# The first two tiles of the feed-forward block's closing projection: one after the other, or side by side

## The chip, the cores and the metric

The kernel runs on one NeuronCore of a Trainium2 chip. The metric is the device time of one execution in microseconds (us), lower is better. TensorE multiplies matrices, VectorE and ScalarE work elementwise, GpSimd here only subtracts, SyncE issues the weight loads.

## What is computed

Two layers of a streaming encoder over 640 tokens (512 of a prompt and 8 streams of 16), width 1024. Each layer holds two half-step feed-forward blocks (FFN) around a mixer:

```
def half_swiglu(x, g, w_up, w_down):
    h = rms_norm(x, g)
    a, b = jnp.split(h @ w_up, 2, axis=-1)
    return x + 0.5 * ((jax.nn.silu(a) * b) @ w_down)

def layer(x, ...):
    x = half_swiglu(x, ffn1_norm, ffn1_up, ffn1_down)
    ...   # sparse attention and a gated convolution, gated, projected, added to x
    x = half_swiglu(x, ffn2_norm, ffn2_up, ffn2_down)
```

`w_down` is 2816 x 1024. The change concerns the last part of `(silu(a) * b) @ w_down`, which is run four times: twice in each layer.

## The kernel before

All values are kept feature-major: 128 features on the partitions, the 640 tokens along the free axis, as two halves of 320. Matrix products are computed in float32 precision from two fp32r parts of each operand: `passes` issues, for one block of 128 x 128 weights, three products (hi x hi, hi x lo, lo x hi) over both halves, so six matmuls. The hidden width of 2816 is 22 blocks. The first 18 are handled by jobs with a seven-product scheme (`jobs`, `product`, names M1 to M7), which TensorE, ScalarE and VectorE work off in an order written out by hand. The last four blocks of the hidden width (`LAST` = 4, `LAST_AT` = 18) are added by plain tiles: this is the closing projection, called "closing" below. It has eight tiles (`KB` = 8), one for each 128 output features, and each tile sums four blocks: 4 x 6 = 24 matmuls into the PSUM buffer `lin[0]` (even tiles) or `lin[1]` (odd tiles).

Around the closing each engine follows its own written order, and semaphores join them:

- **TensorE** (`ffn`, lines 995 to 1005) runs a loop of four rounds with two tiles each. Before a tile it waits until the tile two back has left PSUM (`evacuated`) and until the tile's weights are there in both parts (`lo_ready`). In even tiles it also waits, before the third and the fourth block, for the hidden block itself (`g_ready`). The fourth hidden block is the last thing that the jobs make: VectorE's `lo_g` (line 2045) writes its low part `g_lo`.
- **ScalarE** (`closing`, line 1272) does for each tile j: `split` (line 1252) the weights of tile j + 2 into `w_hi`, then wait for `x` of tile j, then write the high part of the next norm's input `h_hi` (line 1257) and the square `sq` (line 1266). The weights have two buffers, so tile k + 2 overwrites the buffer of tile k:

```
            def split(L, k, i=0, step=2, cols=KB * P):
                s = k % 2
                act.wait_ge(tile_done.sem, L * TILES + (k - 1) + (step * i))
                ...
                nc.scalar.activation(w_hi[:, s, 0:cols], w_raw[:, s, 0:cols], ACT.Copy).then_inc(hi_ready.sem, 1)
```

- **GpSimd** (`low`, line 588) then subtracts, `w_lo = w_raw - w_hi`, and signals `lo_ready`.
- **SyncE** (`load`, line 528) loads `w_raw` of tile k once `w_lo` of tile k - 2 is made.
- **VectorE** (`closing`, line 1856) does for each tile: add it to `x` out of PSUM (line 1868), make `h_lo` (line 1821), and add `sq` into `acc` (line 1832). In the last closing of all, `h_hi` and `h_lo` fall away. In the second closing (layer 0, second FFN) VectorE and ScalarE also prepare the first job of the next layer in between: after tile 3 VectorE adds two weight strips (`add_strips` S1, S2, line 1907), after tile 4 two more (S3 and `first_fourth`), and ScalarE writes their high parts (line 1308).

After tile 7 comes the next stage's first tile, whose weights (1024 columns) go through the same `split` and `low`.

Of the kernel before, what the change touches and what calls it, by code (L numbers as in the profile page):

```python
# [37 lines left out]
KB = D_MODEL // P  # L38
TT = T // P
FB = D_FF // P  # L40
# [15 lines left out]
LAST = GROUPS[SPLIT_GROUPS]  # L56
LAST_AT = FB - LAST
# [119 lines left out]
def build(nc, wts, x_in, gains_in, cos_in, sin_in, ident_in, bmask_in, convw_in, state_in,  # L177
          kcache_in, vcache_in, kidx_in, y_out, k_out, v_out, ki_out, conv_out):
    ctx = ExitStack()
    with ctx:  # L180
# [109 lines left out]
        last_hi = [g_hi[:, i, :] for i in range(LAST)]  # L290
        last_lo = [g_lo[:, i, :] for i in range(LAST)]
# [46 lines left out]
        def res(slot):  # L338
            return lin[slot][:, :, 0:HALF]
# [16 lines left out]
        lo_ready = Signal("lo_ready", TILES)  # L356
        tile_done = Signal("tile_done", TILES)
        evacuated = Signal("evacuated", RESULTS, 2)
# [37 lines left out]
        g_ready = Signal("g_ready", 2 * FB)  # L396
# [319 lines left out]
        def _(pe):  # L716
            def passes(out, s, c, rhs_hi, rhs_lo, first, last):

                whi, wlo = w_hi[:, s, c * P:(c + 1) * P], w_lo[:, s, c * P:(c + 1) * P]
                for n, (w, a) in enumerate(((whi, rhs_hi), (whi, rhs_lo), (wlo, rhs_hi))):  # L720
                    for half in range(2):
                        ins = nc.tensor.matmul(out[:, half, :], w, a[:, half * HALF:(half + 1) * HALF],  # L722
                                               start=first and n == 0, stop=last and n == 2)
                return ins

            def linear(L, n, m, s, hi, lo, blocks=KB, before_last=None, out=None, after_block=None, frees_rows=False):

                out = res(s) if out is None else out

                pe.wait_ge(evacuated.sem, evacuated.count(L, m - 1))  # L730
                pe.wait_ge(lo_ready.sem, lo_ready.count(L, n + 1))
                for c in range(blocks):
                    if before_last and c == blocks - 1:
                        before_last()
                    ins = passes(out, s, c, hi[:, c, :], lo[:, c, :], c == 0, c == blocks - 1)
                    if after_block:
                        after_block()
                    if frees_rows and c == 3:
                        ins.then_inc(first_rows_free.sem, 1)
                ins.then_inc(tile_done.sem, 1)  # L740

            def first_linear(L, n, m, p):


                s = n % 2
                pe.wait_ge(evacuated.sem, evacuated.count(L, m - 1))
                pe.wait_ge(lo_ready.sem, lo_ready.count(L, n + 1))
                for c in range(KB):
                    if c == SUM_BEFORE:
                        sum_squares(L, p)  # L750
                    pe.wait_ge(h_ready.sem, h_ready.count(L, (p - 1) * KB + c + 1))
                    ins = passes(res(m % 2), s, c, h_hi[:, c, :], h_lo[:, c, :], c == 0, c == KB - 1)
                ins.then_inc(tile_done.sem, 1)
# [94 lines left out]
            def second_linear(L, n, m, p):  # L848

                blocks = iter(range(KB))  # L850

                def after_block():
                    if next(blocks) == SPREAD_AFTER:
                        spread_r(L, p)
                linear(L, n, m, n % 2, h_hi, h_lo, out=res(m % 2), after_block=after_block)
# [113 lines left out]
            def jobs(L, f, q, m):  # L969

                first_job(L, f, q, m)
                for k in range(2, NJ):
                    m1(L, q + k)
                    m4(L, q + k - 1)
                    m6(L, q + k)
                    m3(L, q + k - 1)
                    m2(L, q + k)
                    m7(L, q + k)
                    m5(L, q + k)
                m4(L, q + NJ - 1)  # L980
                pe.wait_ge(g_made.sem, g_made.count(L, ups(f, NJ - 2)))
                m3(L, q + NJ - 1)

            def ffn(L, f, n0, m0):
                q = f * NJ
                if L == f == 0:
                    opening_pair()
                else:
                    first_linear(L, n0, m0, (0, 2)[f])
                    second_linear(L, n0 + 1, m0 + 1, (0, 2)[f])  # L990
                for k in range(2, 2 * PLAIN):
                    linear(L, n0 + k, m0 + k, k % 2, h_hi, h_lo, frees_rows=k == 2 * PLAIN - 1)
                n0, m0 = n0 + 2 * PLAIN, m0 + 2 * PLAIN
                jobs(L, f, q, m0)
                with pe.Fori(0, KB // 2) as i:

                    pe.wait_ge(g_ready.sem, g_ready.count(L, f * FB + FB - 2))
                    for s in range(2):
                        pe.wait_ge(evacuated.sem, evacuated.count(L, m0 + s - 1 + 2 * i))
                        pe.wait_ge(lo_ready.sem, lo_ready.count(L, n0 + s + 1 + 2 * i))  # L1000
                        for c in range(LAST):
                            if s == 0 and c >= LAST - 2:
                                pe.wait_ge(g_ready.sem, g_ready.count(L, f * FB + LAST_AT + c + 1))
                            ins = passes(res(s), s, c, last_hi[c], last_lo[c], c == 0, c == LAST - 1)
                        ins.then_inc(tile_done.sem, 1)

# [104 lines left out]
            for _ in range(WARM_UP):  # L1111
                nc.tensor.matmul(bank[:, 3, :], ones[:, 0:1].to_broadcast([P, P]), ones[:, 0:1].to_broadcast([P, 512]),
                                 start=True, stop=True)
            for L in range(DEPTH):
                ffn(L, 0, FFN1_AT, 0)

                first_linear(L, MIX_AT, MIX_RES, 1)
# [112 lines left out]
                with pe.Fori(0, KB // 2) as i:  # L1230
# [5 lines left out]
                    for s in range(2):  # L1236
                        linear(L, OUT_AT + s + 2 * i, OUT_RES + s + 2 * i, s, m_hi, m_lo,
                               before_last=last_sum if s == 0 else None)
                ffn(L, 1, FFN2_AT, FFN2_RES)

            sum_last_squares()
# [1516 lines left out]
```

## Time and profile before

| | |
|---|---|
| device time, median of 3 runs | 2693.67 us (2692.46 to 2694.69) |
| the profiled execution: its own time | 2693.38 us |
| its span, first to last instruction | 2691.6 us |
| mean granted TensorE clock | 0.998 |
| TensorE busy | 2649.7 us (98%) |
| VectorE, ScalarE, GpSimd busy | 2050.8, 1347.4, 1014.6 us |

The profiled execution's own time is 1.8 us more than its span, for what lies before the first and after the last instruction. The trace names instructions by engine, line and tile. Matmuls overlap: one takes 0.31 us from start to end, but they start 0.147 us apart, so a duration is read from starts. A line "x2" of the timeline merges two matmuls. The closings begin at 409.55, 1315.50, 1741.08 and 2647.03 us of the span.

### The profile page before, as it was taken

To read this page: it belongs to the slowest core of one execution; us is meant where nothing else is said; L and a number is where in the kernel's file an instruction comes from. 1 tells how busy PE (TensorE), PEld (TensorE's weight loads), DVE (VectorE), ACT (ScalarE), POOL (GpSimd) and SP (SyncE) were. 2 spreads that over 40 slices of the span, in tenths; PEclk is the share of its full clock that TensorE was granted. 3 is DMA by queue.
4 is the path that set the end of the run, shared out by engine and by line. 5 is a ranking of instruction groups with operands and counts; after the bars stand their busy time and mean duration, and the time that the engine had idled before them with its cause. 6 is when DMAs were issued, how large, how long until landed. Compare 5 with 4: busy or idle time off the path is not lost. (4 is left out here: it accounts for less than half of the span.)

```text
span 2691.6 us, 48351 instructions
## 1 busy us (share of the span) xinstructions
PE 2649.7 (98%) x18372; PEld 2584.3 (96%) x18372; DVE 2050.8 (76%) x3441; ACT 1347.4 (50%) x2498; POOL 1014.6 (38%) x690
## 2 busy tenths in 40 slices
PE   9999999999999999999999999999999999999997
PEld 8999999998999999999999999998989999999997
DVE  8998976886433699989689889668773347989985
ACT  5555555636322355555545555464463224555553
POOL 2343333345433333343333433333544333343432
PEclk9999999999999999999999999999999999999999
DMA  3222223233222222232212222222332221222222
GB/s 120 79 95 92 74 79 98 88 126 126 64 70 94 70 68 98 69 104 80 79 65 93 77 98 79 76 92 89 133 111 71 70 94 63 77 97 79 91 83 71
DMA packets 89783, 234.27 MB, mean 87 GB/s; under 512 B 8816, under 2 KB 42352, under 8 KB 89072
## 3 DMA queue, kind: packets, MB, share of 16 engines
q1 hardware_dynamic: 74784, 204.11, 23.0%
q10 hardware_dynamic: 14800, 27.51, 3.0%
q8 instruction: 125, 2.05, 0.3%
q14 instruction: 74, 0.61, 0.1%
HBM read 223.32 MB, written 8.27 MB: 86 GB/s over the span
## 5 line engine op out<-in xcount | busy, mean ns | idle before, releaser
L588 POOL TENSOR_TENSOR w_lo<-w_raw,w_hi 128x1024 fp32r<-128x1024 f32 (+1 forms) x190 | 403.3, 2123 | 679.4 <-ACT w_hi L1252 663.5
L642 POOL TENSOR_TENSOR lo_A<-raw_odd,hi_A 128x512 fp32r<-128x512 f32 (+1 forms) x180 | 277.5, 1541 | 476.9 <-ACT hi_A L1308 476.6
L1252 ACT ACTIVATE w_hi<-w_raw 128x1024 fp32r<-128x1024 f32 (+1 forms) x174 | 168.7, 970 | 470.7 <-PE lin L722 341.5
L642 POOL TENSOR_TENSOR lo_A<-raw_even,hi_A 128x512 fp32r<-128x512 f32 (+1 forms) x180 | 247.4, 1375 | 399.9 <-ACT hi_A L1308 398.8
L722 PE MATMUL lin<-h_hi,w_hi 128*128 128x320 f32 x1600 | 374.6, 315 | 5.0 <-DVE tmp L1808 2.7
L722 PE MATMUL lin<-h_hi,w_lo 128*128 128x320 f32 x1600 | 365.2, 309 | 0.0
L722 PE MATMUL lin<-h_lo,w_hi 128*128 128x320 f32 x1600 | 364.8, 309 | 0.0
L722 PEld LDWEIGHTS lin<-h_hi,w_hi 128*128 128x128 f32 x1600 | 265.6, 189 | 18.6 <-issue 14.0
L722 PEld LDWEIGHTS lin<-h_lo,w_hi 128*128 128x128 f32 x1600 | 267.9, 188 | 0.0
L722 PEld LDWEIGHTS lin<-h_hi,w_lo 128*128 128x128 f32 x1600 | 267.8, 188 | 0.0
L887 PE MATMUL bank<-h_hi,hi_A 128*128 128x320 f32 x704 | 217.8, 309 | 1.1 <-DVE h_lo L2058 0.7
L887 PE MATMUL bank<-h_hi,lo_A 128*128 128x320 f32 x704 | 217.5, 309 | 0.0
L887 PE MATMUL bank<-h_lo,hi_A 128*128 128x320 f32 x704 | 217.5, 309 | 0.0
L1308 ACT ACTIVATE hi_S<-lin 128x512 fp32r<-128x512 f32 (+1 forms) x240 | 130.3, 553 | 127.9 <-DVE lin L1907 65.8
L1917 DVE TENSOR_TENSOR lo_S<-lin,hi_S 128x512 fp32r<-128x512 f32 (+1 forms) x240 | 150.6, 629 | 13.0 <-ACT hi_S L1308 11.2
L887 PE MATMUL bank<-T_hi,hi_S 128*128 128x320 f32 x480 | 148.4, 309 | 1.0 <-DVE lo_S L1917 1.0
L887 PE MATMUL bank<-T_hi,lo_S 128*128 128x320 f32 x480 | 148.3, 309 | 0.0
L887 PE MATMUL bank<-T_lo,hi_S 128*128 128x320 f32 x480 | 148.3, 309 | 0.0
L1308 ACT ACTIVATE hi_A<-raw_even 128x512 fp32r<-128x512 f32 (+1 forms) x192 | 112.8, 588 | 59.7 <-PE lin L887 36.0
L1308 ACT ACTIVATE hi_A<-raw_odd 128x512 fp32r<-128x512 f32 (+1 forms) x180 | 105.2, 584 | 63.1 <-PE bank L887 61.7
L887 PEld LDWEIGHTS bank<-h_hi,hi_A 128*128 128x128 f32 x704 | 132.1, 188 | 1.7 <-DVE h_lo L2058 1.6
L887 PE MATMUL lin<-T_hi,hi_S 128*128 128x320 f32 x432 | 133.5, 309 | 0.0
(418 smaller groups left out, 7794.9 us busy)
## 6 DMA issues: line engine op xcount, KB each, us to landing
w_raw<-wts SPq DMA_DIRECT2D x144, 512.0 KB, 3.5
raw_even<-wts SPq DMA_DIRECT2D x80, 512.0 KB, 4.3
raw_odd<-wts SPq DMA_DIRECT2D x72, 512.0 KB, 4.1
raw_even<-wts SPq DMA_DIRECT2D x48, 384.0 KB, 3.7
raw_odd<-wts SPq DMA_DIRECT2D x48, 384.0 KB, 3.7
w_raw<-wts SPq DMA_DIRECT2D x32, 256.0 KB, 2.6
caches<-kcache_in ACTq DMA_DIRECT2D x16, 512.0 KB, 4.1
caches<-vcache_in ACTq DMA_DIRECT2D x16, 512.0 KB, 4.9
```

Source lines behind the costliest of these rows:

```text
L588: ins = nc.gpsimd.tensor_tensor(w_lo[:, s, cols], w_raw[:, s, cols], w_hi[:, s, cols].bitcast(F), ALU.subtract)
L642: nc.gpsimd.tensor_tensor(strip_lo[name][:, cols], raw_pair[k % 2][:, block_, cols], strip_hi[name][:, cols].bitcast(F), ALU.subtract).the ...
L722: ins = nc.tensor.matmul(out[:, half, :], w, a[:, half * HALF:(half + 1) * HALF], start=first and n == 0, stop=last and n == 2)
L887: ins = nc.tensor.matmul(out, w[i][:, c * P:(c + 1) * P], a[j], start=opens and c == n == 0, stop=c == blocks - 1 and n == 2, skip_group_c ...
L1252: nc.scalar.activation(w_hi[:, s, 0:cols], w_raw[:, s, 0:cols], ACT.Copy).then_inc(hi_ready.sem, 1)
L1308: nc.scalar.activation(strip_hi[name][:, cols], src, ACT.Copy).then_inc(strip_hi_done[name].sem, 1)
L1917: nc.vector.tensor_tensor(strip_lo[name][:, cols], src, strip_hi[name][:, cols].bitcast(F), ALU.subtract).then_inc(strip_ready[name].sem, 1)
```

## The change

The first two tiles of each closing are taken out of the loop. Blocks 0, 1 and 2 of tile 0 are run, then blocks 0, 1 and 2 of tile 1, then, after one wait for the fourth hidden block, block 3 of tile 0 and block 3 of tile 1. Both tiles accumulate at the same time, in `lin[0]` and `lin[1]`. The loop does the other six tiles in three rounds, without waits for `g_ready`. Nothing is changed on the other engines.

```
-                with pe.Fori(0, KB // 2) as i:
-
-                    pe.wait_ge(g_ready.sem, g_ready.count(L, f * FB + FB - 2))
+                for s in range(2):
+                    pe.wait_ge(evacuated.sem, evacuated.count(L, m0 + s - 1))
+                    pe.wait_ge(lo_ready.sem, lo_ready.count(L, n0 + s + 1))
+                    for c in range(LAST - 1):
+                        if s == 0:
+                            pe.wait_ge(g_ready.sem, g_ready.count(L, f * FB + LAST_AT + c + 1))
+                        passes(res(s), s, c, last_hi[c], last_lo[c], c == 0, False)
+                pe.wait_ge(g_ready.sem, g_ready.count(L, f * FB + FB))
+                for s in range(2):
+                    passes(res(s), s, LAST - 1, last_hi[LAST - 1], last_lo[LAST - 1], False, True).then_inc(tile_done.sem, 1)
+                n0, m0 = n0 + 2, m0 + 2
+                with pe.Fori(0, KB // 2 - 1) as i:
+
                     for s in range(2):
                         pe.wait_ge(evacuated.sem, evacuated.count(L, m0 + s - 1 + 2 * i))
                         pe.wait_ge(lo_ready.sem, lo_ready.count(L, n0 + s + 1 + 2 * i))
                         for c in range(LAST):
-                            if s == 0 and c >= LAST - 2:
-                                pe.wait_ge(g_ready.sem, g_ready.count(L, f * FB + LAST_AT + c + 1))
                             ins = passes(res(s), s, c, last_hi[c], last_lo[c], c == 0, c == LAST - 1)
                         ins.then_inc(tile_done.sem, 1)
```

## Rows read from the trace of the kernel before

**Rows 1.** The page: span, busy us of the engines, one DMA issue (KB, us to landing).

```profile
span 2691.6 us, 48351 instructions
...
PE 2649.7 (98%) x18372; PEld 2584.3 (96%) x18372; DVE 2050.8 (76%) x3441; ACT 1347.4 (50%) x2498; POOL 1014.6 (38%) x690
...
w_raw<-wts SPq DMA_DIRECT2D x32, 256.0 KB, 2.6
```

**Rows 2.** Who TensorE waited for: us in total, times, longest us.

```profile
PE lin L887 <- DVE tmp L1932: 8.1, 8, 1.2
...
PE lin L722 <- DVE g_lo L2045: 2.8, 4, 0.7
```

**Rows 3.** Timeline of TensorE, second closing: start us, duration us, instruction, idle before.

```profile
1315.50 0.46 PE L722 MATMUL lin<-g_hi,w_hi 128*128 128x320 f32 x2
...
1319.01 0.56 PE L722 MATMUL lin<-g_hi,w_hi 128*128 128x320 f32 x2 [0.71 <-DVE g_lo L2045]
...
1319.98 0.46 PE L722 MATMUL lin<-g_hi,w_hi 128*128 128x320 f32 x2
...
1323.50 0.46 PE L722 MATMUL lin<-g_hi,w_hi 128*128 128x320 f32 x2
...
1341.17 0.57 PE L722 MATMUL lin<-g_hi,w_hi 128*128 128x320 f32 x2
...
1346.74 0.53 PE L722 MATMUL lin<-h_hi,w_hi 128*128 128x320 f32 x2 [1.78 <-issue]
```

**Rows 4.** Timeline of ScalarE, second closing.

```profile
1320.18 0.63 ACT L1252 ACTIVATE w_hi<-w_raw 128x512 fp32r<-128x512 f32 x1 [2.09 <-PE lin L722]
```

**Rows 5.** Timeline of GpSimd, second closing.

```profile
1320.89 1.30 POOL L588 TENSOR_TENSOR w_lo<-w_raw,w_hi 128x512 fp32r<-128x512 f32 x1 [7.39 <-ACT w_hi L1252]
...
1334.97 1.70 POOL L588 TENSOR_TENSOR w_lo<-w_raw,w_hi 128x512 fp32r<-128x512 f32 x1 [2.21 <-ACT w_hi L1252]
1339.37 1.75 POOL L588 TENSOR_TENSOR w_lo<-w_raw,w_hi 128x512 fp32r<-128x512 f32 x1 [2.71 <-ACT w_hi L1252]
1343.74 2.90 POOL L588 TENSOR_TENSOR w_lo<-w_raw,w_hi 128x1024 fp32r<-128x1024 f32 x1 [2.62 <-ACT w_hi L1252]
```

**Rows 6.** Timeline of VectorE, second closing.

```profile
1318.13 0.83 DVE L2045 TENSOR_TENSOR g_lo<-tmp,g_hi 128x640 fp32r<-128x640 f32 x1 [0.81 <-ACT g_hi L1373]
...
1320.25 0.82 DVE L1868 SCALAR_TENSOR_TENSOR x<-lin,x 128x640 f32<-128x640 f32 x1 [0.60 <-PE lin L722]
...
1330.74 0.82 DVE L1868 SCALAR_TENSOR_TENSOR x<-lin,x 128x640 f32<-128x640 f32 x1
...
1334.10 0.68 DVE L1907 TENSOR_TENSOR S_sum<-raw_even 128x512 f32<-128x512 f32 x1
1334.81 0.69 DVE L1907 TENSOR_TENSOR S_first<-S_sum,raw_even 128x512 f32<-128x512 f32 x1
1335.42 0.82 DVE L1868 SCALAR_TENSOR_TENSOR x<-lin,x 128x640 f32<-128x640 f32 x1
...
1338.67 0.68 DVE L1907 TENSOR_TENSOR raw_even<-raw_even 128x512 f32<-128x512 f32 x1
```

**Rows 7.** Timeline of VectorE in the middle of the jobs.

```profile
1080.42 0.69 DVE L1907 TENSOR_TENSOR S_sum<-raw_odd 128x512 f32<-128x512 f32 x1
1081.14 1.67 DVE L1907 TENSOR_TENSOR lin<-S_sum,raw_odd 128x512 f32<-128x512 f32 x1
```

**Rows 8.** Timeline of GpSimd in the middle of the jobs.

```profile
1080.89 1.36 POOL L642 TENSOR_TENSOR lo_A<-raw_odd,hi_A 128x512 fp32r<-128x512 f32 x1 [4.25 <-ACT hi_A L1308]
```

**Rows 9.** Third closing, TensorE, at its end.

```profile
1770.54 0.53 PE L722 MATMUL lin<-h_hi,w_hi 128*128 128x320 f32 x2 [0.17 <-issue]
```

**Rows 10.** Third closing, GpSimd, at its end.

```profile
1768.02 2.42 POOL L588 TENSOR_TENSOR w_lo<-w_raw,w_hi 128x1024 fp32r<-128x1024 f32 x1 [2.64 <-ACT w_hi L1252]
```

**Rows 11.** Stages of the span: busy us of each engine, PEclk granted, DMA share, GB/s.

```profile
1347.70:1350.90 3.20, 3.20 (x14) 3.20 (x13) 2.30 (x4) 1.47 (x3) 0.00 (x0) 0.50 0.44 154
...
1019.00:1022.40 3.40, 2.19 (x15) 1.92 (x14) 3.33 (x5) 0.44 (x1) 2.00 (x2) 1.00 0.10 9
```

## The prediction, made before the changed kernel was run

> **What bounds the kernel now.** I read the page first: TensorE is busy for 98% of a span of 2691.6 us [rows 1], so a gain has to come out of its few waits. The list of those waits has one that this change is aimed at: four waits for `g_lo` of line 2045, 2.8 us together, 0.7 us each [rows 2]. Then the timeline of one closing. I take the second (layer 0, second FFN) and count from its first matmul at 1315.50; the other three have the same starts up to the third tile within 0.02 us. Tile 0 ends, and tile 1 begins, at 4.48; tile 1 takes 3.52 and tile 2 begins at 8.00 [rows 3]. Without a wait a tile is 3.52 us, a block 0.88. So the wait costs 4.48 - 3.52 = 0.96 us of TensorE's issue, not the 0.71 beside the row: the last matmuls are still draining when the idle time begins (about 0.15), and the first pair after a wait takes 0.56 instead of 0.46 (0.10) [rows 3]. All of this is on the path: nothing else can start.
>
> What does tile 2 wait for? Not for hidden blocks but for its weights, whose buffer is that of tile 0. ScalarE's split starts at 4.68, which is 0.20 after tile 0's end [rows 4]; GpSimd's subtraction starts at 5.39 and ends at 6.69 [rows 5], 2.21 after tile 0's end. Tile 2 begins at 8.00, so this chain has 1.3 us of slack today. The change moves the end of tile 0, and that is the point to work out.
>
> **Part 1: the wait for `g_lo` goes.** `g_lo` ends at 1318.96, 3.46 after the start [rows 6]. The fourth block of tile 0 now comes after six blocks, at 6 x 0.88 = 5.28. The wait is met 1.8 us early and costs nothing. If only this counted, each closing would win 0.96 us. The other new waits are on things already there (blocks 18 to 20 and the weights of tile 1 were ready in time before), and the loop's end and entry show no gap today. Costed at nothing; the cover is TensorE's queue of issued matmuls.
>
> **Part 2: tile 0 ends later.** It ends at 5.28 + 0.88 = 6.16 instead of 4.48 (+1.68), tile 1 at 7.04 instead of 8.00. The weights' chain is unchanged, so `w_lo` of tile 2 is ready at 6.16 + 2.21 = 8.37. From GpSimd's end to the matmul it releases there is 0.05 us (1339.37 + 1.75 to 1341.17) to 0.10 (1343.74 + 2.90 to 1346.74) [rows 3, 5]; I take 0.05. Tile 2 starts at 8.42, its first pair slow by 0.10, so it ends as if begun at 8.52. That is 0.52 later than the 8.00 of before; with the bounds 0.45 to 0.60. TensorE stands idle from about 7.2 to 8.42, 1.2 us instead of 0.7. The wait is not removed but changed into a longer one, for GpSimd instead of VectorE.
>
> **What is late next.** Tile 3's split is queued on ScalarE behind `h_hi` and `sq` of tile 0, which wait for x of tile 0: it begins near 8.7, its `w_lo` ends near 10.9, and tile 3 starts at 12.04: 1.1 us of cover. x of tile 1 must have left `lin[1]`: VectorE does it at 9.7 to 10.5, covered. SyncE's load for tile 4 is issued after `w_lo` of tile 2, at 8.4, takes 2.6 us [rows 1] and is wanted at 12.2: 1.1 us of cover. In the first and the third closing VectorE has caught up by tile 6, and the next stage is released by `w_lo` of its 1024-column weights (third closing: GpSimd ends 1768.02 + 2.42 = 1770.44, matmul at 1770.54 [rows 9, 10]), which follows the end of tile 6: +0.52 is carried on. In the fourth, too: everything behind tile 7 follows it. Three closings: 3 x 0.52 = 1.56 us.
>
> **The second closing is different.** There VectorE sets the pace from tile 4 on. Its x of tile 0 starts 0.27 after the tile's end: now 6.43 instead of 4.75 [rows 6]. When it need not wait for TensorE, VectorE takes 3.25 us a tile (1335.42 to 1338.67 [rows 6]), against TensorE's 3.52, so it recovers only 0.27 a tile: x of tile 3 starts at 6.43 + 3 x 3.25 = 16.18 instead of 15.24. The strip sum S1 follows 3.25 later, 19.43 to 20.11 (before 18.60). Now the order against GpSimd matters. Before, S2 was asked for at 19.31 and GpSimd's `w_lo` at 19.47; GpSimd's took 1.70 instead of 1.30 [rows 5, 6]. After, `w_lo` of tile 6 is asked for 0.91 after tile 4's end at 8.52 + 3 x 3.52 = 19.08, so at 19.99, while S1 runs, and S2 only at 20.14. In the middle of the jobs just this order shows: S1 at 1080.42, GpSimd at 1080.89, S2 at 1081.14, and S2 takes 1.67, until 0.56 after GpSimd's end [rows 7, 8]. So here GpSimd ends at 20.11 + 1.17 = 21.28 (1.17 as at 1335.50 to 1336.67 [rows 5, 6]), S2 at 21.84, x of tile 4 starts 0.08 before that, at 21.76 instead of 19.92: +1.84 us. From there on the closing hangs on VectorE and ScalarE: x of tile 4, ScalarE's strips, the split and `w_lo` of tile 7 (tile 7 starts with GpSimd's end [rows 3, 5]), then those of the next stage, which starts at 1346.74 after 1.78 us idle [rows 3]. I carry +1.84 through. If S2 is asked for first, x of tile 4 starts at 20.14 + 0.61 = 20.75, only +0.83.
>
> The Trainium skill says the same of this port (SBUF — State Buffer, "Who interferes with whom"): a VectorE instruction with two SBUF inputs and a reading GpSimd instruction exclude each other, and the first to issue keeps the port to its end. By that rule x out of PSUM, with one SBUF input, is not held up. The sum would be the same 1.84 by it.
>
> **The sum.** 1.56 + 1.84 = 3.40 us on the profiled execution's own 2693.38 us (span 2691.6 and 1.8 around it): 2696.8 us. The median of the runs shown is 0.29 higher, 2693.67; against it this is +0.12%. What can be told from no change is 0.2%, 5.4 us: the forecast is a slowdown that lies within it.
>
> **The rivals.**
> - *S2 comes first.* For it: the two requests are 0.15 us apart, the size of my errors. Then 1.56 + 0.83 = 2.4: 2695.8 us.
> - *The clock's dip of the second closing is lost.* After the 1.78 us idle the granted clock is 0.50, which is 1.2 GHz, for 3.2 us [rows 11]; six pairs took 3.2 us instead of 1.76, some 1.5 us lost. Idle of up to 1.2 us, in eight waits for line 1932 [rows 2], did not: in the stretch behind the one at 1019 TensorE is busy for only 2.19 of 3.4 us, at a granted clock of 1.00 [rows 11]. The idle time before the next stage stays, but a new one of 1.2 to 1.4 us comes before tile 7, and whether the clock falls could change. Without the dip: 2695.3 us, with S2 first 2694.3.
> - *The clock falls behind the new idle time.* Each dip costs 1.5 us. Against it: idle of the same 1.2 us left the clock at 1.00 [rows 11]. Two dips more make 6.4 us: 2699.8, past the 0.2%; four make 2702.8. This is the case on the slow side that could be measured.
> - *The wait goes and none comes.* That would need `w_lo` of tile 2 by 7.04, so within 0.88 us of tile 0's end; the split alone takes 0.63 and the subtraction 1.30 [rows 4, 5]. Gain 4 x 0.96 = 3.8: 2689.5 us, faster, still within 0.2%; with the dip lost as well 2688.0, just beyond it.
>
> **How the numbers follow.** My forecast 0.45; S2 first 0.18; the dip lost, in either order, 0.20; the clock falling more often 0.07; no new wait 0.04; the rest, something not seen, 0.06. The runs before spread over 2.2 us, so a median may be off by 1 us either way. The range goes from the dip lost with S2 first (2694.3 less 0.5) to the upper bound of Part 2 and some 1.7 for a stretch or dip not counted: 2693.8 to 2698.8. Faster by over 0.2% (below 2688.3) takes the last rival with the lost dip: 0.02. Slower by over 0.2% (above 2699.1) takes two dips or more: 0.07. Within: 0.91.
>
> **What would show it.** In the changed profile: no wait for `g_lo` of line 2045; four waits of about 1.2 us at the first matmul of tile 2, with GpSimd's `w_lo` ending 0.05 before; the split of tile 2 at 6.36 after the closing's start; in the second closing S2 at some 1.7 us, x of tile 4 at 21.8, tile 7 at 27.5. I would be wrong if tile 2 started at 7.04 (then the weights do not hang on tile 0's end), if the second closing lost no more than the others (then VectorE's lag is not what carries), or if the granted clock showed more than one dip.

## The result, and the profile after

The changed kernel takes 2698.43 us (median of 20 runs, 2694.98 to 2702.14) against 2693.57 us (20 runs, 2692.02 to 2696.04): a ratio of 1.0015, 95% interval 1.0009 to 1.0022. It is slower, by less than the 0.2% set as the bound of what counts as a difference. The forecast was 2696.8 us, with a range from 2693.8 to 2698.8; the median is 1.6 us above the forecast and 0.4 us inside the upper end of the range. Eight of the 20 runs lie above it. The profiled execution took 2697.01 us, of which the span is 2695.2.

The page first: span and busy time, for [rows 1].

```profile
span 2695.2 us, 48319 instructions
...
PE 2650.8 (98%) x18372; PEld 2585.9 (96%) x18372; DVE 2046.7 (76%) x3441; ACT 1347.0 (50%) x2498; POOL 1015.7 (38%) x690
```

TensorE does the same number of matmuls in a span that is 3.6 us longer. Who TensorE waited for (us in total, times, longest), for [rows 2]:

```profile
PE lin L887 <- DVE tmp L1940: 8.1, 8, 1.2
...
PE lin L722 <- POOL w_lo L588: 5.8, 5, 1.3
```

All lines of the other engines have moved down by 8: L1932 is L1940 now. The wait for `g_lo` is gone from the list, and a wait for `w_lo` has come. Four of its five are the first matmuls of tile 2; the fifth is tile 7 of the second closing. The timeline of TensorE in the second closing, for [rows 3]:

```profile
1316.36 0.46 PE L722 MATMUL lin<-g_hi,w_hi 128*128 128x320 f32 x2
...
1323.11 0.46 PE L722 MATMUL lin<-g_hi,w_lo 128*128 128x320 f32 x2
1324.75 0.56 PE L722 MATMUL lin<-g_hi,w_hi 128*128 128x320 f32 x2 [1.18 <-POOL w_lo L588]
...
1343.84 0.57 PE L722 MATMUL lin<-g_hi,w_hi 128*128 128x320 f32 x2 [0.99 <-POOL w_lo L588]
...
1349.43 0.53 PE L722 MATMUL lin<-h_hi,w_hi 128*128 128x320 f32 x2 [1.80 <-issue]
```

Counted from 1316.36, tile 2 starts at 8.39 (8.42 was expected), tile 7 at 27.48 (27.5) and the next stage at 33.07, where it was 31.24. ScalarE and GpSimd, for [rows 4, 5]:

```profile
1322.72 0.63 ACT L1260 ACTIVATE w_hi<-w_raw 128x512 fp32r<-128x512 f32 x1 [3.77 <-PE lin L722]
```

```profile
1323.43 1.26 POOL L588 TENSOR_TENSOR w_lo<-w_raw,w_hi 128x512 fp32r<-128x512 f32 x1 [9.07 <-ACT w_hi L1260]
...
1336.32 1.33 POOL L588 TENSOR_TENSOR w_lo<-w_raw,w_hi 128x512 fp32r<-128x512 f32 x1 [2.22 <-ACT w_hi L1260]
```

The split starts at 6.36, 0.20 after the end of tile 0, and `w_lo` ends at 8.33; the matmul follows 0.06 later. VectorE, for [rows 6]:

```profile
1318.99 0.82 DVE L2053 TENSOR_TENSOR g_lo<-tmp,g_hi 128x640 fp32r<-128x640 f32 x1 [0.81 <-ACT g_hi L1381]
...
1322.79 0.82 DVE L1876 SCALAR_TENSOR_TENSOR x<-lin,x 128x640 f32<-128x640 f32 x1 [2.28 <-PE lin L722]
...
1335.81 0.69 DVE L1915 TENSOR_TENSOR S_sum<-raw_even 128x512 f32<-128x512 f32 x1
1336.53 1.67 DVE L1915 TENSOR_TENSOR S_first<-S_sum,raw_even 128x512 f32<-128x512 f32 x1
1338.12 0.81 DVE L1876 SCALAR_TENSOR_TENSOR x<-lin,x 128x640 f32<-128x640 f32 x1
```

GpSimd's subtraction starts at 1336.32, while S1 still runs (1335.81 to 1336.50) and just before S2 (1336.53), so S2 takes 1.67 us instead of the 0.69 of [rows 6], and x of tile 4 starts at 21.76 instead of 19.92.

Stage by stage, from each closing's first matmul to the first of the next stage (after the fourth: of the last stage, L844): 29.45 to 29.99, 31.24 to 33.07, 29.46 to 29.94, 34.36 to 34.86. That is +0.54, +1.83, +0.48 and +0.50: 3.35 us, where the prediction's sum was 3.40.

The stretch from the start to the first closing is 0.2 us longer (409.55 to 409.75). No changed instruction has run there yet, but the granted clock has: in this execution it fell to half once near the start (busy us of PE, PEld, DVE, ACT, POOL with their instruction counts, granted clock, DMA share, GB/s), where the kernel before has 1.00:

```profile
9.30:12.70 3.40, 3.36 (x12) 3.29 (x13) 2.09 (x2) 3.40 (x6) 2.38 (x1) 0.50 1.05 400
```

What the profile does not explain is that the medians stand 4.9 us apart. Most experiments after the first two are about that.

### The profile page after: what moved, and what is told of

Its sections match the earlier page's. It is cut to its first block and busy times, and to the rows that moved or that the text cites. A ratio compares the mean times of both kernels' runs of the same rounds, so it can differ in the third digit from the quotient of the medians.

```text
span 2695.2 us, 48319 instructions
## 1 busy us (share of the span) xinstructions
PE 2650.8 (98%) x18372; PEld 2585.9 (96%) x18372; DVE 2046.7 (76%) x3441; ACT 1347.0 (50%) x2498; POOL 1015.7 (38%) x690
```

## The experiments

Each was timed in 11 runs, beside runs of the kernel before on the same chip. In the first group (e1 to e4) the kernel before took 2693.99 us (median of 33 runs, 2692.41 to 2697.72), in the second (e5 to e8) 2694.10 (33 runs, 2691.79 to 2698.98), in the third (e9) 2694.86 (15 runs, 2692.29 to 2697.88). The difference between these kernels and the spread of one are of one size, so the mean of the runs is given where it matters, in places with a 95% interval worked out from the spread of the runs.

**e1: the changed kernel once more.** No edit.

> The changed kernel once more, beside the others. Both theories: 3 to 6 us above the kernel before. Theory A (the wait for tile 2's weights costs 0.5 us in three closings and 1.84 us in the second, and the rest of the loss is a granted clock that falls in more of the executions, behind the new idle time): the runs with the lower mean clock are the slower ones, some 1.5 us for each fall, and the spread over runs is wider than that of the kernel before. Theory B (the clock has nothing to do with it): the spread is that of before, and time does not follow the clock.

Measured: 2696.02 us (2695.47 to 2699.95), ratio 1.0012 (1.0003 to 1.0021), mean 2697.27. The median is 2.4 us lower than the first time, and the runs fall into two groups: six with a mean granted clock of 0.998 at 2695.47 to 2696.02, five at 0.996 with 2698.48 to 2699.95. The 20 runs of the result go the same way: four at 0.998 with a median of 2695.47, seven at 0.997 with 2697.30, eight at 0.996 with 2699.44, one at 0.995 with 2702.14. A median of such a mixture lands in one group or the other. In means the difference to the kernel before is 4.35 us in the first measurement and 3.25 here, over all 31 runs 3.96. Theory A was right that the slower runs are those with the lower clock; where the clock falls is a question for the profiles. The profiled execution of e1 (2695.65 us) has the closings of the first one (30.00, 33.07 and 29.94 us for the first three), but no fall at all before TensorE's last few matmuls: neither the one near the start nor the one behind the second closing. The third closing begins 393.34 us after the second ends, where it was 394.20 in the first profile and 394.34 in the kernel before, so the fall behind the second closing costs 0.9 to 1.0 us. That is less than its length suggests, because without it TensorE waits 0.60 us for `acc` at the first matmuls of L772:

```profile
1353.80 0.48 PE L772 MATMUL bank<-acc,ones 128*32 128x160 f32 x8 [0.60 <-DVE acc L1840]
```

**e2: S2 ahead of GpSimd.** In the second FFN of layer 0, GpSimd's subtraction for tile 6 waits until S2 is done.

```
+                    if k == 6 and f == 1 and L < DEPTH - 1:
+                        pool.wait_ge(sums_done["S2"].sem, sums_done["S2"].count(L + 1, 1))
                     low(L, n + k, all_cols=LAST * P)
```

> GpSimd's subtraction for tile 6 of the second closing also waits for VectorE's strip sum S2, so that S2 is first at the port. If the order of the two requests cost 1.0 us there: S2 takes 0.7 us instead of 1.67, x of tile 4 starts 20.8 us after the closing's start instead of 21.8, the next stage starts at 32.1 instead of 33.1, and the kernel is 1.0 us faster than the changed one. If only VectorE's lag counts (rival), x of tile 4 stays at 21.8 and the time is that of the changed kernel.

Measured: 2695.32 us (2694.64 to 2700.32), ratio 1.0007 (0.9998 to 1.0016), mean 2696.68. VectorE's timeline, with the closing's first matmul at 1318.39 and lines 2 further down than in the changed kernel:

```profile
1338.57 0.69 DVE L1917 TENSOR_TENSOR S_first<-S_sum,raw_even 128x512 f32<-128x512 f32 x1
1339.18 0.82 DVE L1878 SCALAR_TENSOR_TENSOR x<-lin,x 128x640 f32<-128x640 f32 x1
```

and GpSimd's:

```profile
1339.34 1.30 POOL L588 TENSOR_TENSOR w_lo<-w_raw,w_hi 128x512 fp32r<-128x512 f32 x1 [3.21 <-DVE S_first L1917]
```

S2 is back at 0.69 us, x of tile 4 starts at 20.79 (changed kernel 21.76), and the next stage at 32.10 instead of 33.07: 0.97 us. GpSimd now starts 1 us later than before the edit, and nothing is the worse for it. So the extra loss of the second closing is, for more than half, the order of these two instructions; the rest is VectorE's lag. The 0.7 us in the median and 0.6 in the mean by which e2 is below e1 is of the right sign, but the runs are too few to size it: the 95% interval of the difference in means goes from 2.4 us faster to 1.3 slower.

This profiled execution is worth more for something else. It took 2700.32 us, the longest of its 11. Its stages show why (columns as above):

```profile
114.40:117.70 3.30, 3.30 (x15) 3.30 (x14) 3.20 (x7) 0.78 (x2) 0.00 (x0) 0.55 0.61 158
1022.40:1025.70 3.30, 3.30 (x15) 3.30 (x15) 3.20 (x7) 0.65 (x2) 0.00 (x0) 0.56 0.66 212
1449.00:1452.30 3.30, 3.30 (x13) 3.30 (x14) 3.21 (x6) 0.49 (x1) 0.34 (x1) 0.55 0.53 181
2357.00:2360.30 3.30, 3.30 (x14) 3.30 (x15) 3.20 (x7) 0.51 (x2) 0.23 (x1) 0.56 0.57 198
...
1326.90:1330.20 3.30, 3.30 (x23) 3.30 (x24) 2.40 (x4) 2.02 (x4) 1.59 (x1) 1.00 0.24 79
```

The granted clock falls to half (1.2 GHz) four times, for some 3.4 us, once in each FFN (0.55 in the rows, whose edges do not quite meet the fall's; 1021.90 to 1025.30 has 0.50) and each time at the same place: behind the waits for `tmp` and `bank` in the middle of the jobs, in job 4 of 0 to 8. In such a stretch TensorE does about 14 matmuls instead of 23. The last row is the stretch behind the closing's new idle time of 1.19 us: clock 1.00, 23 matmuls. TensorE at the second of these places:

```profile
1019.19 0.41 PE L889 MATMUL bank<-g_sums_hi,hi_S 128*128 128x320 f32 x1 [0.99 <-ACT bank L1330]
...
1021.99 0.63 PE L889 MATMUL lin<-h_hi,hi_S 128*128 128x320 f32 x1 [1.22 <-DVE tmp L1942]
1022.42 0.47 PE L889 MATMUL lin<-h_lo,hi_S 128*128 128x320 f32 x1
1022.68 0.47 PE L889 MATMUL lin<-h_hi,lo_S 128*128 128x320 f32 x1
1022.95 0.47 PE L889 MATMUL lin<-h_hi,hi_S 128*128 128x320 f32 x1
```

Two waits within 3 us, and behind the second each matmul starts 0.27 us after the last, where 0.147 is usual. Nine matmuls fewer in a stretch are 9 x 0.147 = 1.3 us; four such falls cost some 5.3 us, and 2700.3 less that is 2695.0, close to this kernel's shortest run (2694.64). The profiles bear the price out: from the third closing's end to the fourth's start this execution takes 877.98 us and e1, without the fall, 876.60, so 1.4 us.

**e3: the new idle time filled.** Eight matmuls into a free part of `bank` between tile 1 and tile 2 of each closing; their result is not used.

```
+                for _ in range(8):
+                    nc.tensor.matmul(bank[:, 3, 0:HALF], last_hi[0][:, 0:P], last_hi[1][:, 0:HALF], start=True, stop=True, ...)
                 n0, m0 = n0 + 2, m0 + 2
```

> Eight matmuls of 320 columns whose result nobody reads, 1.17 us together, stand between tile 1 and tile 2 of each closing, where TensorE waits anyway. Tile 2 still starts when its weights are ready. Theory A: the granted clock no longer falls behind this place, the spread over runs shrinks to that of the kernel before, and the median is the mechanism's 3.4 us above the kernel before (3.0 to 3.8). Theory B: no change against the changed kernel's median, or slower by what the eight matmuls push out.

Measured: 2698.35 us (2695.84 to 2700.20), ratio 1.0014 (1.0005 to 1.0023), mean 2698.24. Tile 2 starts at 8.42 to 8.52, as in the changed kernel. No lower in the median, 1 us higher than e1 in the mean. If the new idle time made the clock fall, filling it would have narrowed the runs down to 2695.5, and it did not. The profiles say the same more directly: in those of the changed kernel (both), of e2 and of e6 below, tile 2 of every closing waits 1.2 to 1.3 us, 16 times in all, and the clock falls behind none of them. The profiled execution again shows two falls in job 4 (at 114 and 1022) and one at 1353, behind the second closing.

**e4: one block between.** Tile 1 has only its first block ahead of the fourth block of tile 0: blocks 0, 1, 2 of tile 0, block 0 of tile 1, block 3 of tile 0, blocks 1, 2, 3 of tile 1. `g_lo` is waited for behind four blocks, at 3.52.

```
-                    for c in range(LAST - 1):
+                    for c in range(LAST - 1 if s == 0 else 1):
...
-                for s in range(2):
-                    passes(res(s), s, LAST - 1, last_hi[LAST - 1], last_lo[LAST - 1], False, True).then_inc(tile_done.sem, 1)
+                passes(res(0), 0, LAST - 1, last_hi[LAST - 1], last_lo[LAST - 1], False, True).then_inc(tile_done.sem, 1)
+                for c in range(1, LAST):
+                    ins = passes(res(1), 1, c, last_hi[c], last_lo[c], c == 0, c == LAST - 1)
+                ins.then_inc(tile_done.sem, 1)
```

> Only one block of tile 1 stands between the third and the fourth block of tile 0. Tile 0 then ends at about 4.4 us instead of 6.16, its successor's weights are ready at 6.6, and tile 2 starts at 7.04, right behind tile 1. If the late end of tile 0 is the cause, all of the 0.96 us is won in each closing: 3.8 us faster than the kernel before, 2689.8 us. In the second closing S2 is then asked for just ahead of GpSimd (18.38 against 18.51); if it is not, 1 us less is won. If running the two tiles side by side costs by itself (two open sums, the code outside the loop), it is not faster than the kernel before.

Measured: 2690.61 us (2689.61 to 2692.65), ratio 0.9987 (0.9978 to 0.9996), mean 2690.73. Neither wait is left; of the pause in issue at the fourth block 0.10 remains. The end of tile 0 is at 4.50, as before the change, so tile 2's weights come as early as before (`w_lo` at 6.70), and tile 2 starts at 7.13, right behind tile 1 (second closing, first matmul at 1314.03):

```profile
1319.43 1.30 POOL L588 TENSOR_TENSOR w_lo<-w_raw,w_hi 128x512 fp32r<-128x512 f32 x1 [7.40 <-ACT w_hi L1262]
1321.16 0.46 PE L722 MATMUL lin<-g_hi,w_hi 128*128 128x320 f32 x2
```

Each closing is shorter than before the change: 28.58 for 29.45, 30.45 for 31.24, 28.59 for 29.46, 33.49 for 34.36, so -0.87, -0.79, -0.87, -0.87, together 3.40 us. S2 is asked for at 18.52 in the second closing, 0.08 ahead of GpSimd, and takes 0.69, GpSimd 1.77:

```profile
1332.55 0.69 DVE L1917 TENSOR_TENSOR S_first<-S_sum,raw_even 128x512 f32<-128x512 f32 x1
1332.63 1.77 POOL L588 TENSOR_TENSOR w_lo<-w_raw,w_hi 128x512 fp32r<-128x512 f32 x1 [2.23 <-ACT w_hi L1262]
```

The gain is 3.4 us and not the 3.8 expected, because of the 0.10 that remains in each closing. Both waits can be taken away at once, and two open sums cost nothing by themselves; the change put two blocks too many ahead.

**e8: two blocks between.** As e4, with blocks 0 and 1 of tile 1 ahead of the fourth block of tile 0, so that tile 0 ends at 5.28.

```
-                    for c in range(LAST - 1 if s == 0 else 1):
+                    for c in range(LAST - 1 if s == 0 else 2):
...
-                for c in range(1, LAST):
+                for c in range(2, LAST):
```

> Two blocks of tile 1 between the third and the fourth block of tile 0. Tile 0 ends at 5.28, its successor's weights are ready at 7.49, tile 2 starts at 7.54 to 7.6, its first pair slow: 0.36 us faster than before in three closings. In the second closing x of tile 3 comes at 15.3 as before, but GpSimd asks at 19.11 while S1 runs (18.55 to 19.23) and S2 at 19.26: S2 takes 1.67 and x of tile 4 comes at 20.9 instead of 19.9. Sum: 0.1 us faster than before, no difference. If the order at the port does not matter: 1.4 us faster.

Measured: 2694.77 us (2691.94 to 2696.96), ratio 1.0001 (0.9992 to 1.0010), mean 2694.59, against a mean of 2694.52 of the kernel before beside it. Tile 2 starts at 7.54; the closings change by -0.29, +0.97, -0.38 and -0.36. The second one, VectorE and then GpSimd:

```profile
1333.88 0.68 DVE L1917 TENSOR_TENSOR S_sum<-raw_even 128x512 f32<-128x512 f32 x1
1334.60 1.67 DVE L1917 TENSOR_TENSOR S_first<-S_sum,raw_even 128x512 f32<-128x512 f32 x1
1336.20 0.81 DVE L1878 SCALAR_TENSOR_TENSOR x<-lin,x 128x640 f32<-128x640 f32 x1
```

```profile
1334.41 1.32 POOL L588 TENSOR_TENSOR w_lo<-w_raw,w_hi 128x512 fp32r<-128x512 f32 x1 [2.22 <-ACT w_hi L1262]
```

GpSimd is 0.19 ahead of S2, which again takes 1.67: here three closings gain, one pays, and nothing is left, as expected.

**e7: the weights of tiles 2 and 3 in a place of their own.** The block order is the change's (three blocks of each tile, then the fourth of each), but the 512 columns of tile 2 and 3 go to the free second half of each weight buffer, and ScalarE splits them ahead of the norm of tile 0, without waiting for a tile's end.

```
-                    load(L, n1 + j, ..., cols=LAST * P)
+                    load(L, n1 + j, ..., cols=LAST * P, at_=LAST * P if j in (2, 3) else 0)
...
-                act.wait_ge(tile_done.sem, L * TILES + (k - 1) + (step * i))
+                if not at_:
+                    act.wait_ge(tile_done.sem, L * TILES + (k - 1) + (step * i))
...
+                    if j == 0 and cols == LAST * P:
+                        split(L, n0 + 2, cols=cols, at_=LAST * P)
+                        split(L, n0 + 3, cols=cols, at_=LAST * P)
```

> The changed kernel, but the weights of tiles 2 and 3 get buffers of their own (the unused second halves), so that they need not wait for tiles 0 and 1. If the shared buffer is what makes the late end of tile 0 expensive, tile 2 starts right behind tile 1, 7.04 us after the closing's start: 0.96 us less than before in three closings. In the second, VectorE still begins 1.7 us later than before, and GpSimd's request comes before VectorE's last acc of tile 3: x of tile 4 at 21.9, 1.9 us later than before. Sum 2693.1 us by means. If the port plays no part there, x of tile 4 is at 20.8 and the sum is 2692.0. If side by side costs by itself, tile 2 starts late all the same.

Measured: 2695.78 us (2692.79 to 2697.65), ratio 1.0001 (0.9992 to 1.0010), mean 2695.70. Tile 2 starts at 7.31, so the 1.2 us wait is gone when the buffer is, which shows that it was the buffer of tile 0 that held tile 2 back. It starts at 7.31 and not at the 7.04 expected, because now it waits for tile 0's sum to leave `lin[0]`: x of tile 0 ends at 1324.03, 7.25 after the start.

```profile
1323.21 0.82 DVE L1888 SCALAR_TENSOR_TENSOR x<-lin,x 128x640 f32<-128x640 f32 x1 [1.79 <-PE lin L723]
1324.09 0.57 PE L723 MATMUL lin<-g_hi,w_hi 128*128 128x320 f32 x2
```

So the other three closings are 0.58 to 0.60 shorter than before the change, where 0.96 was expected. The second is 1.95 longer, because S1 now runs into GpSimd:

```profile
1336.23 1.78 DVE L1927 TENSOR_TENSOR S_sum<-raw_even 128x512 f32<-128x512 f32 x1
...
1338.66 0.82 DVE L1888 SCALAR_TENSOR_TENSOR x<-lin,x 128x640 f32<-128x640 f32 x1
```

```profile
1335.89 1.58 POOL L589 TENSOR_TENSOR w_lo<-w_raw,w_hi 128x512 fp32r<-128x512 f32 x1 [1.66 <-ACT w_hi L1269]
```

The x of tile 4 comes at 21.88, as late as in the changed kernel. By its closings the kernel should be 0.2 us slower than before in total; I had expected 1 us faster. Its mean is 1.2 us above the kernel before beside it, with a 95% interval from 0.1 faster to 2.4 slower. Its profiled execution had falls of the clock at 9.8, 1020.2, 1351.3 and 2354.8.

**e5 and e6: the waits of job 4 filled**, in the kernel before (e5) and in the changed one (e6), the same edit in both: 7 and 9 matmuls of 192 columns, result not used, into a free part of `bank`, ahead of the two products of job 4 that wait.

```
+                def filler(n):
+                    for _ in range(n):
+                        nc.tensor.matmul(bank[:, 3, HALF:512], h_hi[:, 0, 0:P], h_hi[:, 0, 0:512 - HALF], start=True, stop=True, ...)
...
                     m4(L, q + k - 1)
+                    if k == 4:
+                        filler(7)
                     m6(L, q + k)
+                    if k == 4:
+                        filler(9)
                     m3(L, q + k - 1)
```

> The kernel before, with 7 and 9 matmuls of 192 columns that nobody reads put into the two longest waits of the jobs (in job 4 of each block, at about 113, 1018, 1443 and 2351 us, idle 1.0 and 1.2 us). In the profiles so far the granted clock fell behind these places, in one execution behind all four, and not behind the new idle time of the closing. Theory A2 (the spread, and the part of the median loss above 3.4 us, come from these falls, which the change moves against the chip's own rhythm but does not cause): the median is 0 to 1 us lower than the kernel before, no execution has a mean clock of 0.996 or below. Rival B: nothing changes, or slower by up to 1 us for the matmuls put in.

> The changed kernel with the same matmuls in the waits of the jobs. Theory A2: the two groups of executions near 2695.7 and 2699 become one, the mean clock is 0.997 or more in all of them, and the median lies 3.4 us (3.0 to 3.8) above that of the kernel before with the same filling. Rival (the new idle time of the closing makes the clock fall): the spread stays and the difference of the two filled kernels is 4 us or more.

Measured: e5 2692.51 us (2691.41 to 2694.03), mean 2692.57; e6 2696.55 (2695.21 to 2697.20), mean 2696.49. Both are below what they were without filling (means of 2694.52 beside them, and of 2697.87 over the 31 runs of the changed kernel), although TensorE is given more to do, and their runs lie closer: a standard deviation of 0.77 us for 1.62 in the kernel before, 0.54 for 1.82 in the 20 runs of the changed one. None of these 22 runs has a mean clock of 0.996 or less, where 14 of the 81 runs of the kernel before in this section have one and 14 of the 31 of the changed kernel. So the falls of the clock behind job 4's waits make most of the spread of these kernels, and they are there before the change as well as after it. The changed kernel has more of them; why is not shown, and as the first of these places (at 114 us) stands before any changed instruction has run, the new idle time cannot be the cause of that one. With job 4's falls taken out of both, the change costs 4.04 us by medians and 3.92 by means (95% interval about 3.3 to 4.5).

Neither expectation was met as it stood. Filling gained 2.0 us by means in the kernel before (1.6 by medians), where at most 1 was expected. In the changed kernel the two groups became one, as Theory A2 said, but the difference of the two filled kernels is above its 3.0 to 3.8, and a difference of 4 or more was the rival's sign; the rival's other sign, the unchanged spread, is absent.

**e9: e4 and the filled job.** One block between, with the filler of e5.

> One block of tile 1 between the third and the fourth block of tile 0, and the idle time in job 4 filled as in the two kernels before. If the two gains add: 3.4 us (four closings) and 1.5 us (mean of the falls of the clock) off the kernel before, median 2689.2 us, no execution with a mean clock below 0.997. If the filling only helped by where the falls came in those two kernels: 2690.6 us, as with one block alone.

Measured: 2688.79 us (2688.45 to 2689.87), ratio 0.9979 (0.9970 to 0.9988), mean 2689.04 against 2694.73 of the kernel before beside it. This beats both kernels: 5.7 us below the kernel before and some 9 below the changed one, and its runs span 1.4 us, none with a mean clock below 0.997: the two gains add, as expected (2689.2).

## Why the prediction was right

**The wait for `g_lo` goes.** As said; the row is gone, and the fourth block of tile 0 follows the third of tile 1 without a pause.

**A longer wait takes its place.** As said: w_lo of tile 2 at 8.33 (8.37 expected), tile 2 at 8.39 to 8.47 (8.42), three closings at +0.54, +0.48, +0.50 (0.52 each). That tile 0's end is what tile 2 hangs on was an argument from the buffers; e7, e8 and e4 showed it. With the buffer taken away tile 2 starts at 7.31, and with tile 0's end moved to 5.28 and 4.50 it starts at 7.54 and without a wait. The rival in which no new wait comes is out by the profile; its price of 0.96 us a closing was also too high, since e7 shows that `lin[0]` is not free before 7.25.

**The second closing.** +1.83 (1.84 expected), x of tile 4 at 21.76, tile 7 at 27.48. The order of S2 and GpSimd, 0.15 us apart in the prediction and 0.21 in the trace, was the least certain step, and it came out as forecast; e2 turned it round by hand and got 20.79 and 32.10, where the rival's reckoning gave 20.75. The rule of the Trainium skill that stood beside this step (SBUF — State Buffer, "Who interferes with whom") agrees in both directions here: S2 takes 1.67 us when GpSimd was first, GpSimd 1.70 [rows 5] and 1.77 (e4) when S2 was. The x of tile 4, which reads PSUM, takes its usual 0.82 us in e2 while GpSimd's subtraction runs (1339.18 and 1339.34).

**The clock.** The forecast kept the fall behind the second closing and added none behind the new idle time. In the changed profile the fall is there (first row, which starts 0.6 us after it), and the stretch behind the new idle time of the first closing has 1.00 (second row), for [rows 11]:

```profile
1351.30:1354.60 3.30, 3.30 (x16) 3.30 (x15) 2.40 (x4) 2.46 (x4) 0.00 (x0) 0.57 0.25 93
...
418.30:421.70 3.40, 3.40 (x24) 3.40 (x25) 2.50 (x4) 2.13 (x4) 1.59 (x1) 1.00 0.23 80
```

e3 shows that without that idle time the times are no lower. But three things in this part did not hold. "More than one dip" was named as a sign of being wrong, and the changed profile has two: the second is the one at 9.3 to 12.7. It comes 400 us ahead of the first changed instruction, so it says nothing against the mechanism, but the sign as it was worded came true. The fall behind the second closing was priced at 1.5 us and costs 0.9 to 1.0; that it was kept was luck, for e1 and e6, with the same closings, were profiled without it. And the argument against more falls was weaker than it looked. It rested on a stretch in job 4 that holds a wait of 1.2 us and has a clock of 1.00 [rows 11], and just behind that wait, in other executions of the same code, the clock does fall. One profiled execution can't show how often.

**The size.** The sum was 3.40 us, and the two profiled executions differ by 3.6: 0.2 before the first closing and 3.35 in the closings. Over many runs the difference comes out larger, 3.96 us in means over 31 runs and 3.92 with job 4 filled in both, but 3.40 lies inside the 95% intervals of both (about 3.2 to 4.7 and 3.3 to 4.5). So it is not shown that the sum was too small; that a part of 0.5 us is missing stays possible. The profiles of e5 and e6 have the same four steps in the closings (+0.55, +1.83, +0.50, +0.49, together 3.37), and nearly all of the 4.05 us by which they differ can be placed: beside the closings 1.08 more before the first, 0.87 less between the second and the third (e5 has the fall behind the second closing and e6 has not) and 0.36 more after the last. The 1.08 arises in the first 15 us, where both run the same instructions: the first matmul of L798 starts at 13.8 in e5 and 14.9 in e6. Over all eleven profiled executions it starts at 13.8 to 14.0 in six and at 14.7 to 15.0 in five, the changed kernel having both (14.90 in the result's profile, 14.03 in e1). So the start, too, varies by about 1 us from execution to execution.

The other 1 us by which the medians differ (4.9 for 3.9) is the mixture: the changed kernel's 20 runs had more executions with falls, and their median fell into the upper group, while in e1 it fell into the lower. The prediction allowed 1 us of error for the median from a spread of 2.2 us in three runs. Twenty runs spread over 7.2 us. That is the step that was mis-sized, and that the median stayed 0.4 us inside the range owes something to luck. The rival "the clock falls more often, 1.5 us each" was about right on the price (1.4 in job 4) and wrong on the place.

## What to carry to other kernels

A reordering that lets one tile start early also moves the end of another, and whatever waits for that end (here the buffer of the tile after next) moves with it: work out the shortest reordering that covers the wait, for one block in between gave 3.4 us, two gave nothing and three cost 3.4. Where two engines ask for the same port 0.2 us apart, treat their order as a part of the change: it was worth 1 us here, and it can be fixed with one wait. And before a difference of 0.1% is explained, sort the runs by their granted clock; if they fall into groups, fill the waits that the falls come behind and compare again.

## What the runs showed of the hardware that was not expected

The clock can fall to half behind two waits of 1.0 and 1.2 us within 3 us, in a stream that is otherwise full, in some executions and not in others of the same kernel. The execution that was profiled for e2 had it at the same place in all four FFNs; those of before and after the change had it in none. A fall lasts about 3.4 us, and its price depends on what TensorE would have waited for anyway: 1.4 us in job 4, 0.9 to 1.0 behind the second closing. Filling the waits with matmuls whose result nobody uses made the kernel before 2 us shorter by means (2692.57 for 2694.52, 95% interval 1.2 to 2.7). A single wait of 1.2 to 1.3 us, in the 16 cases above, brought no fall. What decides from execution to execution whether the clock falls was not found.
